# Gate columns of the latent input projection by seven block products in place of eight, with the low parts shared out between GpSimd and VectorE

## What is computed

```python
h = rms_norm(x, norm_g[0])
proj = h @ w_in                      # 1024 x (384 + 256 + 64 + 2048)
c_q, c_kv, k_pe, z = jnp.split(proj, [384, 640, 704], axis=-1)
q  = (rms_norm(c_q,  g_cq)  @ w_uq ).reshape(B, S, 16, 192)
kv = (rms_norm(c_kv, g_ckv) @ w_ukv).reshape(B, S, 16, 256)
...
o = o.reshape(B, S, 16 * 128) * jax.nn.silu(z)
return o @ w_out
```

## Time and profile before

| | |
|---|---|
| median of 3 runs | 958.93 us (957.84 to 960.82) |
| the profiled execution, its own time | 956.71 us |
| its span, first to last instruction | 954.9 us |
| mean granted TensorE clock | 0.993 |
| PE, DVE, ACT, POOL busy | 98%, 50%, 44%, 46% of the span |

### The profile page before, as it was taken

How to read it: one execution, slowest core, us unless ns; L and a number is a source line. 1 busy time by engine, 2 the same in 40 slices (tenths; PEclk the granted TensorE clock), 3 DMA queues, 4 the chain that set the end, 5 groups by cost and what they waited for, 6 DMA issues and landing times. The chain is left out here.

```text
span 954.9 us, 15648 instructions
## 1 busy us (share of the span) xinstructions
PE 933.2 (98%) x5650; PEld 819.9 (86%) x5650; DVE 476.7 (50%) x1587; ACT 419.7 (44%) x973; POOL 441.8 (46%) x589
## 2 busy tenths in 40 slices
PE   6999998999999999999999999999989999999998
PEld 6888888999999997888888877888868999999986
DVE  5231018878778785221111124677736666666621
ACT  5363227777777775322332233443334333333410
POOL 2443427888778763233443254668723211111121
PEclk9999999999999999999999999999979999999999
DMA  6332321110111012122272212232210100000001
GB/s 215 106 128 67 101 81 48 48 41 20 48 49 37 24 46 89 45 89 87 93 151 85 87 52 81 89 95 89 89 45 1 45 2 1 1 1 2 1 34 56
DMA packets 39254, 58.85 MB, mean 62 GB/s; under 512 B 8693, under 2 KB 22282, under 8 KB 39178
## 3 DMA queue, kind: packets, MB, share of 16 engines
q1 hardware_dynamic: 39136, 57.84, 19.4%
q10 hardware_dynamic: 42, 0.01, 0.0%
HBM read 55.62 MB, written 2.10 MB: 60 GB/s over the span
## 5 line engine op out<-in xcount | busy, mean ns | idle before, releaser
L1137 POOL TENSOR_TENSOR w_lo<-w_raw,w_hi 128x2048 fp32r<-128x2048 f32 (+1 forms) x26 | 118.4, 4554 | 158.8 <-ACT w_hi L911 158.8
L95 PE MATMUL bank<-w_hi,h_hi 128*128 128x512 f32 (+2 forms) x480 | 187.2, 390 | 2.9 <-POOL w_lo L1065 1.9
L97 PE MATMUL bank<-w_hi,h_lo 128*128 128x512 f32 (+2 forms) x480 | 183.3, 382 | 0.0
L96 PE MATMUL bank<-w_lo,h_hi 128*128 128x512 f32 (+2 forms) x480 | 183.2, 382 | 0.0
L95 PEld LDWEIGHTS bank<-w_hi,h_hi 128*128 128x128 f32 x480 | 90.2, 188 | 21.3 <-issue 2.6
L97 PEld LDWEIGHTS bank<-w_hi,h_lo 128*128 128x128 f32 x480 | 90.2, 188 | 17.2
L96 PEld LDWEIGHTS bank<-w_lo,h_hi 128*128 128x128 f32 x480 | 90.3, 188 | 15.6
L1798 POOL TENSOR_TENSOR o_c<-o_c,o_sw 128x256 f32<-128x256 f32 x16 | 11.6, 728 | 164.9 <-DVE o_c L1871 164.9
L911 ACT ACTIVATE w_hi<-w_raw 128x2048 fp32r<-128x2048 f32 (+1 forms) x26 | 49.2, 1891 | 78.9 <-PE bank L97 78.9
L1645 PE MATMUL bank<-kvr,probT 128*128 128x65 f32 x640 | 80.6, 273 | 0.0
L1645 PEld LDWEIGHTS bank<-kvr,probT 128*128 128x128 f32 x640 | 78.6, 192 | 1.3
(11 more groups left out here) (274 smaller groups left out, 2175.0 us busy)
## 6 DMA issues: line engine op xcount, KB each, us to landing
w_raw<-in_nsa_w_in SPq DMA_DIRECT2D x10, 1024.0 KB, 5.0
w_raw<-in_mla_w_in SPq DMA_DIRECT2D x8, 1024.0 KB, 5.0
w_raw<-in_mla_w_out SPq DMA_DIRECT2D x8, 1024.0 KB, 5.1
w_raw<-in_nsa_w_in SPq DMA_DIRECT2D x8, 984.0 KB, 5.0
w_raw<-in_mla_w_uq SPq DMA_DIRECT2D x8, 576.0 KB, 4.2
w_raw<-in_mla_w_ukv SPq DMA_DIRECT2D x16, 256.0 KB, 2.7
w_raw<-in_nsa_w_out SPq DMA_DIRECT2D x4, 1024.0 KB, 5.0
w_raw<-in_mla_w_in SPq DMA_DIRECT2D x4, 704.0 KB, 5.7
```

What stands on the lines that cost most here:

```text
L95: nc.tensor.matmul(out, a[0], b[0], start=start, stop=False)
L96: nc.tensor.matmul(out, a[0], b[1], start=False, stop=False)
L97: return nc.tensor.matmul(out, a[1], b[0], start=False, stop=stop)
L1137: nc.gpsimd.tensor_tensor(w_lo[g % 2][:, :, 0:width], w_raw[g % 2][:, :, 0:width], w_hi[g % 2][:, :, 0:width].bitcast(F32), ALU.subtract). ...
```

## The change

The gate columns are computed by a scheme that needs seven block products where the plain way needs eight. One gate chunk of 512 columns is taken as two halves of 256 columns, the 1024 rows as two halves of 512 (the two pieces), and the 512 tokens as two halves of 256. Seven products of one (sum of) token-and-row half of h with one (difference of) weight block are computed, and the four results are made of them by sums.

- PE: a block product (`z_product`) is 2 token tiles x 4 x 3 = 24 matmuls of 256 columns into the two halves of one bank. There are 7 per chunk, 28 in all, 672 matmuls. They are called P0 to P27 here, and block i is the weight block that P(i) needs. The five `turn_c` stand behind P7 to P11.
- Weight blocks: of the seven of a chunk, blocks 0, 4 and 5 are plain quarters of the weights, and blocks 1, 2, 3 and 6 are differences. DVE makes the differences (`w_difference`, 128 x 1024 elements, both operands in SBUF, L1417). ACT makes the high part of each (`block_hi`, 1024 elements, L871). The low part is made by POOL for the three plain blocks (L1208) and by DVE for the four differences (L1401). The high and low buffers are now rings of four quarter blocks, so block i's high part waits for P(i-4).
- Sums of h: ahead of the first product DVE makes four sums of halves of h (`h_sums`), ACT their high parts (`sum_hi`) and DVE their low parts (`sum_lo`).
- Results: ACT copies the first product out of its bank (`z_copy`), DVE adds the others (`z_sums`, seven additions of 128 x 512 per chunk, bank and `z_sb` as operands), and silu is then applied in place in `z_sb` by ACT, eight calls of 256 columns per chunk.
- Moved: `lo(2)` and `lo(3)`, the low parts of chunk 1, from POOL to DVE. The squares of the latent columns (`c_square`) now stand between `block_hi(3)` and `block_hi(7)` on ACT. The scaling by their factors goes from DVE to ACT (`c_scale`), behind `block_hi(8)` and `block_hi(9)`. The rotation of the keys' shared part comes at step 14 of DVE's loop.

The core of the diff:

```diff
+                w_block = [at_raw(0, 0), at_raw(0, 0), w_diff[:, :, :], at_raw(0, 1), at_raw(1, 0), at_raw(1, 1),
+                           w_diff[:, :, :]]
+                is_diff = lambda b: b in (1, 2, 3, 6)
+                h_block = [h_half(0, 0), h_sum[0], h_sum[1], h_sum[2], h_half(1, 0), h_half(0, 1), h_half(1, 1)]
+                by_pool = lambda i: i % 7 in (0, 4, 5)
...
@@ PE
-                    for n in range(1, NCH):
-                        for j in range(2):
-                            pe.wait_ge(a_lo, 2 * n + j)
...
+                    def z_product(q, b):
+                        i = 7 * q + b
+                        if by_pool(i):
+                            pe.wait_ge(z_lo_pool, lows(i, True))
+                        else:
+                            pe.wait_ge(z_lo, lows(i, False))
+                        if q == 0 and b < 4:
+                            pe.wait_ge(c_left, NT + b + 1)
+                        else:
+                            bank_left(bank_user(i))
...
@@ ACT
+                    def block_hi(i):
+                        if i < 2:
+                            act.wait_ge(a_used, NCC)
+                        elif i < 4:
+                            act.wait_ge(a_done, NT * NCC)
+                        else:
+                            act.wait_ge(z_used, i - 3)
...
+                    for p in range(NB + 1):
+                        if p == NB - 2:
+                            split_kv(0)
+                            split_q(0)
+                        if p % 7 == 1:
+                            z_copy(p // 7)
+                        if p == 0:
+                            block_hi(2)
+                            sum_hi(3)
+                        block_hi(p + 3)
+                        if p:
+                            z_leave(p - 1)
+                        if p in (0, 1, 2, 3):
+                            c_square(p)
+                        if p in (5, 6):
+                            c_scale(2 * (p - 5))
+                            c_scale(2 * (p - 5) + 1)
...
@@ POOL
-                    for g in range(2, 6):
-                        lo(g)
+                    block_lo(0)
+                    block_lo(4)
                     pool.wait_ge(c_squared, 3 * NT)
...
-                    for g in range(6, NPC):
-                        lo(g)
+                    for i in range(5, NB):
+                        if by_pool(i):
+                            block_lo(i)
...
@@ DVE
+                    for t in range(NT - 1):
+                        c_leave(0, t)
+                    lo(2)
+                    c_leave(0, NT - 1)
+                    lo(3)
+                    h_sums()
+                    block_lo(0)
+                    w_difference(1)
                     for t in range(NT):
+                        c_leave(1, t)
+                    block_lo(1)
+                    w_difference(2)
+                    block_lo(2)
+                    w_difference(3)
+                    sum_lo(3)
...
+                    for p in range(NB + 1):
+                        if p:
+                            z_sums(p - 1)
+                        if p == NB - 2:
+                            split_kv(0)
+                            split_q(0)
+                        block_lo(p + 3)
+                        w_difference(p + 4)
+                        if 7 <= p < 7 + KQ + KKV:
+                            c_low(p - 7)
+                        if p == 14:
+                            dve.wait_ge(c_factor, 1)
+                            keys_rotate()
```

More of the change, by code:

```diff
@@ L480, in project_q @@
+                    for q in range(NZ):
+                        for b in range(7):
+                            z_product(q, b)
+                            if q == 1 and b < KQ + KKV:
+                                turn_c(b)
                     def project_q(m):
```

332 lines of the change are left out of this document (239 added, 93 removed).

## The result

The changed kernel takes 961.12 us (median of 7, 959.83 to 962.16), the kernel before 957.84 beside it (median of 7, 956.47 to 961.25). The ratio is 1.0034, with a 95% interval of 1.0019 to 1.0049: 3.3 us slower, where +7.0 had been forecast. The direction was right; the size was twice too large. The 961.1 lies inside the stated range of 958.5 to 973, and at the lower edge of the 961 to 970 that the forecast's mechanism had for itself.

The account below looks back on a forecast made before the run. PE, busy 98%, was taken as the bound. Stage end 45.1 + 79.2 + 2.1 (transposes) + 17.7 (losses) = 144.1 against 137.85, 6.3 later; with 0.7 at the heads, 958.9 + 7.0 = 965.9 us, range 958.5 to 973.

Parts of the forecast that it names:

- the forecast's mechanism: Gate chunks: PE's savings are outweighed by waits for late blocks; +3.5 to +11 us (961 to 970), chance 0.62.
- What PE saves: Gate stage: 28 products of 256-column matmuls save 9.9 us, chunk 1 ending earlier saves 1.4; together 11.3.
- Prices and exclusion: Added operations: DVE low part or difference 1.2, POOL low part 2.4, ACT high part 1.06; two-SBUF-operand DVE work excludes POOL's.
- the signs: Changed profile: many of DVE's 1024-element rows far over 1.2 us on average, among other marks.
- the question that the prediction left to a choice: Shared SBUF ports: both DVE and POOL wait (stage end 144.1, taken), or POOL never waits (140.9).
- The first gate chunk: Late blocks on DVE, ACT and POOL: P0 loses 3.5 us, P4 1.3, P5 5.4.
- The 1.4 of P2 and P3: First gate chunk: P2 and P3 lose 0.6 and 0.8 us behind DVE's differences and low parts.
- P19 loses 2.1: Rotation of the keys between POOL's low parts of blocks 18 and 19: P19 waits 2.1 us for its bank.
- P24 to P26 lose 1.9: Last gate chunk: these products lose 1.9 us because DVE is still behind.
- The transposes lose 2.1: Behind P7: PE waits 2.1 us for the scaled latent columns from ACT, behind difference 8 and its high part.
- The 0.7 at the heads: Behind the gate stage: the last sum and two silus delay the heads' start by 0.7 us more.
- DVE becomes the bound in all four chunks: Rival: difference, high and low part take 3.5 us against a product's 2.83; about 975 us, chance 0.13.

Follow-up runs that it names:

- e13: Changed kernel with the rotation of the keys at step 12 in place of 14, where POOL makes no low part; 959.3 us, ratio 1.0014.
- e9: Changed kernel with the rotation of the keys at step 17 in place of 14; 960.8 us, ratio 1.0033.
- e6: Changed kernel with e1's edit and all four latent tiles scaled one step earlier on ACT; 958.9 us, ratio 1.0012.
- e1: Changed kernel with POOL making the low part of block 5 ahead of the latent columns' factors; 960.8 us, ratio 1.0026.
- e14: e6 with the rotation of the keys at step 12 in place of 14; 956.4 us, ratio 0.9978.
- e2: Changed kernel with chunk 1's latent columns leaving between the low parts of the sums of h on DVE; 960.4 us, ratio 1.0026.
- e3: Changed kernel with the edits of e1 and e2 together; 960.0 us, ratio 1.0021.
- e7: e6 with e2's edit and the rotation of the keys at step 12 in place of 14; 956.2 us, ratio 0.9980.
- e15: e5 with e6's early scaling of the four latent tiles on ACT; 958.7 us, ratio 1.0010.
- e16: e6 with product 7, the first of chunk 1, made twice on PE; 959.1 us, ratio 1.0006.
- e5: Changed kernel with the low parts of all seven blocks on DVE, none on POOL; 957.3 us, ratio 0.9990.
- e8b: e5 with e2's order on DVE and e6's early scaling on ACT; 959.5 us, ratio 1.0015.
- e4: Kernel before with only the low parts of chunk 1's two pieces moved from POOL to DVE; 955.4 us, ratio 0.9972.
- e10: e7 with the rotation of the keys at step 17 in place of 12; 957.2 us, ratio 1.0000.
- e12: e6 with the rotation of the keys at step 17 in place of 14; 957.0 us, ratio 0.9997.

## Why the prediction was right in sign and wrong in size

**What PE saves: right.** Matmuls of 256 columns are 0.119 apart, as the 0.118 said. Chunk 1 ends 1.6 earlier (1.4). No engine waits for a DMA between 46 and 143 us, so to count nothing for it was right too.

**Prices and exclusion: right, and met less often than the signs said.** 1.22, 2.38 and 1.06 for 1.2, 2.4 and 1.06. On the question that the prediction left to a choice, POOL's own rows decide: 3.09 beside DVE's work, 2.38 alone. So both wait. The Trainium skill, page SBUF — State Buffer, section "SBUF: two separate sides", says the same, and by that rule the stage would have ended at 144.1; it ended at 142.7, though for another reason.

**The first gate chunk: right in mechanism, with some luck in the numbers.** P0 at 48.6, P4 at 62.5, P5 at 70.9 were forecast at 48.6, 62.5 and 70.8. That they agree to 0.1 is luck, since this trace begins 0.7 later: from the first matmul they start at 34.6, 48.5 and 56.9, and 35.3, 49.2 and 57.5 had been forecast. The losses are 3.1, 0.9 and 5.4 for 3.5, 1.3 and 5.4. The 1.4 of P2 and P3 isn't there as waits: PE ran at 1.2 GHz from 49.9 to 53.1, and again from 71.2 to 73.6, and was late by itself. Those two stretches cost PE 2.8 us in all, and about as much is missing from the waits for P2, P3, P4 and the transposes; so nothing had to be added for the clock, as forecast. e13 and e9 bear that out: their second stretch costs 0.8 and 1.3 more up to P7, and P8 starts within 0.3 of the changed kernel's.

**The step that failed: "P19 loses 2.1" and "P24 to P26 lose 1.9", the 4.0 called the softest.** By the distances of the products they measured 0.8 and 0.9 (P18 to P20 take 0.75 and 0.07 over 2.85, P24 to P26 take 0.36, 0.49 and 0.09 over it).

The first term failed by the lead. The rotation meets POOL's low parts of blocks 18 and 19 as described and holds DVE for 4.3 us more; D17 to D24 is 22.9 against PE's 19.9, 3.0 longer. But PE doesn't lose what DVE loses: it loses what goes beyond DVE's lead, and the wait for block 5, priced in full a few lines before, had given that lead (2.5 us at P17, 0.3 left at P24). I added two losses of which the second was partly paid by the first. e6 is the test: with the wait for block 5 gone and a lead of 0.3 at P17 as at P24, PE takes 22.9 us from P17 to P24, the whole 3.0 more. In e1 that wait is gone too, but PE stands as long in the transposes, the lead is 2.4 and PE loses 0.8: it is standing still that gives the lead, wherever it is.

The second term isn't explained by the lead. It is 0.9 in e6 as well, half of the 1.9, and what P25 and P26 wait for is POOL's low parts (0.20 and 0.22), not a DVE that is behind. From P14 to E the changed kernel takes 41.65 and e6 43.77, where 14 products need 39.9: 1.8 and 3.9 more. So the total of 4.0 would have been about right without a lead, though not its split. Nor is all of e6's 3.9 due to POOL's holding the rotation: e14, where none of its operations is held, still takes 42.15.

**The transposes lose 2.1: too much as well,** 1.0 by the distances of the products. **The 0.7 at the heads: not there.** From E to the heads' gap are 15.3 us in both kernels. ACT's first head square is 1.7 after E in place of 0.9, but before, ACT stood 0.94 for PE ahead of its next square, and now it doesn't: that square is 2.5 after E in both. Timelines of ACT, before and changed:

```profile
140.36 0.33 ACT L847 ACTIVATE sq_junk<-bank 128x192 f32<-128x192 f32 x1 [0.94 <-PE bank L97]
```

```profile
145.22 0.33 ACT L963 ACTIVATE sq_junk<-bank 128x192 f32<-128x192 f32 x1
```

**The sum.** From the first matmul, E was forecast at 144.1 - 13.3 = 130.8 and is 128.7, so 2.1 less. The losses are 3.1 + 0.9 + 5.4 + 1.0 + 1.8 = 12.2 at the waits and 2.8 at half clock, 15.0 for 17.7: 2.7 less, of which 2.2 are the 4.0. Chunk 1 takes off 0.2 more; against that, products of 2.85 for 2.83 add 0.6, and the transposes take 2.2 where the sum had 2.1 (above it the prediction had found 2.3). The remaining 0.1 is rounding. With nothing at the heads, +7.0 becomes +4.2, as the traces say; the medians say +3.3.

**What sets the end, then.** In the five kernels with the rotation at step 14 and POOL's three low parts per chunk (the changed one, e1, e2, e3, e6), P14 starts anywhere from 81.9 to 87.1, and E is 36.7 to 36.8 after D17 in all. There the end goes with DVE's queue and not with PE's place at P14. Where the rotation stands at step 12 (e7, e13, e14), PE waits for nothing from P20 on, P24 starts 1.3 to 1.4 after its low part is done, and PE's own pace sets the end. So the two are close, and what is saved on one soon meets the other.

Three differences in a row take DVE 3.55 each (difference, high part, low part), where PE needs 2.85. That is the chain of the rival "DVE becomes the bound in all four chunks" (3.5 against 2.83). Its price was wrong: the plain blocks behind the differences make up for it, since D17 to D24 is 19.9 in e13, PE's pace. The queue doesn't carry every delay either: in e1 D10 is 2.3 earlier and D17 0.7, because it waits for PE's transposes in between, and D10 to D17 is anything from 21.5 to 25.2 in these kernels. So e2, e1 and e6 gave back most or part of what they won early, at different places; this account fits them, but only e6, e13, e15 and e16 test a part of it.

**Left open.** Why E follows D24 by 15.1 in e5, e8b and e15 and by 13.9 with POOL wasn't followed row by row, nor what ends a wait of 1.92 ahead of P5 in e5, e8b and e15, for which the profile names no releaser. That e4 is 1.3 us faster than its 1.6 was not tested beyond the clock's records. In e7, e10 and e15 chunk 1 itself ended 0.8 later than in the others; this wasn't looked into.

## What to carry to other kernels

When several waits are priced in a row, ask for each whether an earlier one has already given the late engine its lead. Follow the queue that is nearest to setting the pace (here DVE's chain of difference, high part and low part) together with what holds it from outside, and let the fast engine's waits be what is left over. A wait of the busiest engine is a symptom: of six edits that removed one (e1, e2, e6, e9, e12, e15), only e6 gained more than 0.8 us at the stage's end, and e15 lost 2.7, while moving a few small operations of DVE out of POOL's way (e13) gained 1.6. Work spread over DVE and POOL with all operands in SBUF is counted once on a common line, but its order matters more than its length: 1.2 us less per chunk on that line, in the wrong order, made the stage end 7.6 later, a third of it by the clock.

Measure the parts of a change alone. The low parts of chunk 1 on DVE, a side move of this change, gave 0.28% by themselves (e4), and the best orders with seven products gave 0.2% with that move inside.
